# The levels of the gated linear attention over 53 slots instead of 36, in a two-layer encoder kernel

## The reference

```
bcum  = cumsum(log_a)                       # per key channel, log_a = log_sigmoid(...) / 16
a[t,s] = sum_d q[t,d] * k[s,d] * exp(bcum[t,d] - bcum[s,d])     for s <= t
o[t]   = a @ v   (and the part of earlier chunks, by a state)
y      = head_rms(o) * silu(r);  h = h + y @ w_out
```

## Time and profile before

| what | value |
| --- | --- |
| time, median of 3 runs | 2431.05 us (2427.83 to 2432.1) |
| profiled execution: time, span | 2430.49 us, 2428.8 us |
| mean granted TensorE clock | 0.992 |
| PE, DVE, ACT, POOL busy | 98%, 69%, 49%, 6% of the span |
| mean of `w_hi` (L542), `w_lo` (L922) | 1036 ns, 1204 ns |
| mean of the GLA's Exp (L868), of its 36 instructions | 1044 ns |
| GpSimd's subtractions (L490), multiplies (L499) | 72 in 61.7 us, 36 in 57.0 us |
| squares on ScalarE for a head (L853, two), Sqrt (L859) | 626 ns each, 478 ns |
| VectorE's evacuation in v_in (L943), r_in (L947) | 718 ns, 693 ns |

### The profile page before, as it was taken

One profiled execution on the slowest core, in us unless ns is written; L12 is line 12 of the kernel. 1 busy time (PEld: TensorE's weight loads), 2 busy tenths in 40 slices (PEclk: granted clock), 3 DMA queues, 4 the chain that ended last, 5 costly groups with the idle time before them and its releaser, 6 DMA issues.

```text
span 2428.8 us, 50438 instructions
## 1 busy us (share of the span) xinstructions
PE 2373.0 (98%) x19301; PEld 2286.6 (94%) x19301; DVE 1666.8 (69%) x2301; ACT 1198.6 (49%) x1540; POOL 152.7 (6%) x186
## 2 busy tenths in 40 slices
PE   8999989999999999999999899999999999999999
PEld 6998888999999999999999788999999999999998
DVE  5547796677755776577566788586777667766774
ACT  4344645555443444445458445554555445444543
POOL 0000001300000000000000556100000000000000
PEclk9999999999999999999999999999999999999999
DMA  6654455555565556665655333466556656666665
GB/s 180 189 149 124 129 144 124 169 171 190 176 205 183 187 184 194 188 198 180 190 170 165 105 96 97 123 196 205 178 187 199 206 182 206 201 196 193 207 192 164
DMA packets 430509, 420.25 MB, mean 173 GB/s; under 512 B 26067, under 2 KB 428285, under 8 KB 430365
## 3 DMA queue, kind: packets, MB, share of 16 engines
q1 hardware_dynamic: 416448, 415.29, 55.2%
q10 hardware_dynamic: 13932, 3.17, 1.2%
HBM read 416.31 MB, written 2.10 MB: 172 GB/s over the span
## 4 chain that ended last, share of the span: by engine, by line
PE 85%; DVE 7%; ACT 3%; issue 2%; POOL 1%; ACTq 1%; DMA 0%; DVEq 0%
PE ps L1419 26%; PE ps L1417 23%; PE ps L1418 23%; PE ps L1415 6%; DVE w_lo L922 2%; PE ps L1640 1%; ACT w_hi L542 1%; PE ps L1485 1%; PE ps L1484 1%; DVE gl_e L1256 1%; PE ps L1465 1%; POOL gl_e L490 1%; DVE rt L1120 1%; PE ps L1486 1%; DVE rt L1128 1%
## 5 line engine op out<-in xcount | busy, mean ns | idle before, releaser
L1417 PE MATMUL ps<-act_hi,w_hi 128*128 128x272 f32 (+1 forms) x4864 | 1371.1, 282 | 10.6 <-DVE w_lo L922 10.5
L1418 PE MATMUL ps<-act_lo,w_hi 128*128 128x272 f32 (+1 forms) x4864 | 1355.0, 279 | 0.0
L1419 PE MATMUL ps<-act_hi,w_lo 128*128 128x272 f32 (+1 forms) x4864 | 1354.7, 279 | 0.0
L922 DVE TENSOR_TENSOR w_lo<-raw,w_hi 128x1024 fp32r<-128x1024 f32 (+1 forms) x800 | 947.3, 1204 | 487.2 <-ACT w_hi L542 463.0
L542 ACT ACTIVATE w_hi<-raw 128x1024 fp32r<-128x1024 f32 (+1 forms) x797 | 816.4, 1036 | 673.3 <-PE ps L1419 641.2
L1417 PEld LDWEIGHTS ps<-act_hi,w_hi 128*128 128x128 f32 x4864 | 929.7, 191 | 18.8 <-issue 11.2
L1418 PEld LDWEIGHTS ps<-act_lo,w_hi 128*128 128x128 f32 x4864 | 929.7, 191 | 1.5
L1419 PEld LDWEIGHTS ps<-act_hi,w_lo 128*128 128x128 f32 x4864 | 929.2, 191 | 0.0
L1419 PE MATMUL ps<-g_both,w_lo 128*128 128x272 f32 (+1 forms) x1408 | 388.3, 276 | 0.0
L1419 PEld LDWEIGHTS ps<-g_both,w_lo 128*128 128x128 f32 x1408 | 268.2, 190 | 0.0
L1415 PE MATMUL ps<-g_both,w_hi 128*128 128x512 f32 x704 | 231.5, 383 | 0.0
(11 more groups left out here) (241 smaller groups left out, 1330.3 us busy)
## 6 DMA issues: line engine op xcount, KB each, us to landing
raw<-in_ffn_w_up SPq DMA_DIRECT2D x352, 512.0 KB, 4.6
raw<-in_ffn_w_down SPq DMA_DIRECT2D x128, 512.0 KB, 4.3
raw<-in_ab_w_in SPq DMA_DIRECT2D x96, 512.0 KB, 3.8
raw<-in_c_w_in SPq DMA_DIRECT2D x96, 512.0 KB, 3.8
raw<-in_ffn_w_down SPq DMA_DIRECT2D x64, 384.0 KB, 3.9
raw<-in_ab_w_out SPq DMA_DIRECT2D x32, 512.0 KB, 3.5
raw<-in_c_w_out SPq DMA_DIRECT2D x32, 512.0 KB, 4.4
tok<-in_x SPq DMA_DIRECT2D x4, 512.0 KB, 7.8
```

The costliest lines, as they stand in the source:

```text
L922: V.tensor_tensor(w_lo[:, s % 4, 0:kc * 256], raw[:, s % 4, 0:kc * 256], w_hi[:, s % 4, 0:kc * 256].bitcast(F32), ALU.subtract).then_inc(S ...
L1417: mm(o, wh, moving(xh, kk), start=(c == 0 and k == 0), stop=False)
L1418: mm(o, wh, moving(xl, kk), start=False, stop=False)
L1419: ins = mm(o, wl, moving(xh, kk), start=False, stop=end)
```

## The change

The levels get slots of their own in a pattern of three: two with a level, one without. Level v runs in slot 1 + v + v // 2, that is in slots 1, 2, 4, 5, 7, 8, ..., 52, 53. The slots of weighings and of squares are moved to come after their head's levels. The slots of Silu, of the normalisation and of the transposes stay as they are, and so do GpSimd's instructions. The engines' code reads the slot of a level from a table instead of using the slot as the level's number.

```diff
         GL_TICKS = 80
-        UNITS_AT = [([u - 1] if units[u - 1][1] is None else []) + [u] for u in level_units]
+        LEVEL_AT = {1 + v + v // 2: v for v in range(len(level_units))}
+        UNITS_AT = {t: ([level_units[v] - 1] if units[level_units[v] - 1][1] is None else []) + [level_units[v]]
+                    for t, v in LEVEL_AT.items()}
         GL_VT = {4 * (k + 1): (2 * k, 2 * k + 1) for k in range(8)}
-        WEIGH = {9: 0, 10: 1, 11: 2, 13: 3, 18: 4, 19: 5, 21: 6, 22: 7, 27: 8, 29: 9, 30: 10, 31: 11,
-                 36: 12, 37: 13, 38: 14, 39: 15}
-        SQUARE = {14: 0, 23: 1, 34: 2, 41: 3}
+        WEIGH = {15: 0, 17: 1, 18: 2, 19: 3, 29: 4, 30: 5, 31: 6, 33: 7, 42: 8, 43: 9, 44: 10, 45: 11,
+                 55: 12, 56: 13, 57: 14, 58: 15}
+        SQUARE = {21: 0, 35: 1, 47: 2, 60: 3}
 
 # ScalarE
-                    for v in ((0, 1) if t == 0 else (t + 1,)):
-                        if v < len(level_units):
-                            t0, t1 = level_span(units[level_units[v]][1])
-                            act.wait_ge(S("gl_dsub"), v + 1)
-                            act.wait_ge(S("gl_psub"), v + 1)
-                            e = gl_e[:, v % 2, :, :, t0:t1]
-                            A(e, e, ACT.Exp, scale=1.0 / GLA_TAU).then_inc(S("gl_exp"), 1)
+                    if t + 1 in LEVEL_AT:
+                        v = LEVEL_AT[t + 1]
+                        t0, t1 = level_span(units[level_units[v]][1])
+                        act.wait_ge(S("gl_dsub"), v + 1)
+                        act.wait_ge(S("gl_psub"), v + 1)
+                        e = gl_e[:, v % 2, :, :, t0:t1]
+                        A(e, e, ACT.Exp, scale=1.0 / GLA_TAU).then_inc(S("gl_exp"), 1)
 
 # VectorE
-                    for v in ((0, 1) if t == 0 else (t + 1,)):
-                        if v < len(level_units):
-                            sub(v)
-                    if t < len(level_units):
-                        mul(t)
-                    if t >= 1 and t - 1 < len(UNITS_AT):
-                        for u in UNITS_AT[t - 1]:
-                            take(u)
+                    if t + 1 in LEVEL_AT:
+                        sub(LEVEL_AT[t + 1])
+                    if t in LEVEL_AT:
+                        mul(LEVEL_AT[t])
+                    for u in UNITS_AT.get(t - 1, ()):
+                        take(u)
 
 # TensorE
-                    for u in (UNITS_AT[t] if t < len(UNITS_AT) else ()):
+                    for u in UNITS_AT.get(t, ()):
                         unit(u)
```

## The result

The changed kernel takes 2440.45 us (median of 7, 2436.41 to 2443.86) against 2431.16 us (7 runs). The ratio is 1.0039, with a 95% interval of 1.003 to 1.0048. The forecast was 2426.6 us with a range up to 2434.0: wrong in sign and outside the range.

What follows compares the result with a forecast made beforehand. TensorE, busy 98% of the span, was taken as the bound, so only its idle or lower-clock time could be won. Leaving 17.4 us, coming 13.5, net 3.9 off 2430.5: 2426.6 us, range 2421.0 to 2434.0.

Steps and rivals of the forecast that it cites:

- the pair: GpSimd's subtraction for the next level, then its multiply for this one; at odd levels both still fall within one step.
- the size of that pair: At odd levels, 1.34 + 1.34 to 2.15 + 1.82 us against 2.85 on offer; waits sum to 3.95 us.
- The covers: Work before odd levels hides GpSimd's lateness: no wait at 9, 27, 13, 21, 29; 0.3, 0.1, 0.3 at 3, 11, 19.
- The start: At the first levels: level 0 waits 2.6 us in place of 3.63, level 1 waits 1.0 for GpSimd; 3.6 together.
- the 2.03 that stay: Before step 1: TensorE's wait of 2.03 us for k_in's evacuation was to remain unchanged.
- Sqrt and Silu: ScalarE, slots 22, 36, 48: table loads ahead of an Exp soon needed; waits 0.6 (slot 36) and 1.2 (slot 48), sum 1.8.
- Level 34: VectorE, slots 50 to 53: normalisation work and slot 48's delay make multiply 34 late; wait 2.0 us, bounds 0 and 5.
- The clock: TensorE at its lower clock after waits at the start and level 34: 1.2 us, bounds 0 and 2 x 2.3.
- Turns: TensorE turning between kinds of matmul: 9 more turns, each 0 to 0.25 us; 0.7 us together.
- Even levels: GpSimd's 1.7 + 1.8 us fit into 5.8; levels 2, 8, 18, 26 meet an evacuation, 0.3 us together.
- Rival (b): Odd levels all pay today's 0.93 us wait, also behind transposes: 4 us more, 2430; chance 0.18.
- Rival (d): Table loads on ScalarE, slots 22, 36, 48: each of 7 holds it 1.3 us more, 9.1 us, 2435.7; chance 0.02.

Runs made afterwards that it cites:

- experiment 1: Changed kernel with GpSimd multiplying for an odd level before subtracting for the next one, instead of after: 2428.58 us, ratio 0.9989 to the kernel before.
- Experiment 4: Changed kernel with weighings and squares moved so that eleven stand in the slot right before an odd level: 2440.58 us, 1.0042 to the kernel before.
- experiment 7: The changed kernel itself, run and profiled again beside the kernel before: 2442.88 us, ratio 1.0044.
- experiment 5: Changed kernel, GpSimd multiplying first before odd levels, head 1's Silu and normalisation later (head 2's normalisation too): 2422.35 us; squares moved as well: 2416.88 us.
- experiment 2: Changed kernel with VectorE's weight-block split in v_in and r_in replaced by a one-input reciprocal of 176 elements: 2422.28 us, 0.9963 to the kernel before.

## Why the prediction was wrong

- **Where the pair stays** ("GpSimd is not touched, and that is the core"): right, and confirmed by experiment 1. All waits for GpSimd are at odd levels.
- **The step that failed** is the size of that pair: "its upper 2.15 + 1.82, against 2.85 on offer: a wait of 0 to 1.1. ... I take the middle", 3.95 us, with 1.0 for level 1. Measured at the same levels: 13.8. Single waits were 0.4 to 1.8. I had seen that the split now falls beside the subtraction, and took the longest row of before for its price. Two things were wrong with that. The middle was too low: at levels 5, 7 and 23 the pair took 3.8 to 3.9 us, close to my upper 3.97, and they waited 1.37, 1.36 and 1.37. And the bound was no bound: at levels 1, 3, 9, 17, 25 and 27 the pair took 4.0 to 5.1 us. The row of before has one split beside it, and in the changed kernel a second one can fall beside the multiply (2.31 us in place of 1.34 at level 3) or more than one VectorE instruction beside the subtraction. No row of before has such overlaps. From before alone, 2.6 us and one w_lo for each of the two splits that can fall beside the pair would have given 5.0 as the bound, an estimate that levels 3 and 27 reach (5.0 and 5.1).
- **The covers did not cover.** Level 3 behind transposes waited 1.77 (I gave 0.3), levels 9 and 27 behind the extra product 0.73 and 1.33 (I gave nothing). Against a pair of 4.6 to 5.1 us the 0.65 and 1.1 us are too little. Levels 11 and 19 stand behind the same transposes and did not wait: their pairs took 2.6 and 3.1. Levels 13, 21 and 29, behind weighings of 1.4 us, did not wait either, but their pairs took only 3.0, so the weighings were hardly put to the test there. Experiment 4 shows that they cover: its levels 23 and 29, with pairs of 3.9 and 4.0 us and a weighing in front, did not wait.
- **The start**: 0.78 + 1.53, or 2.45 and no wait at level 1 when the clock held (experiment 7). I gave 2.6 + 1.0; the 2.03 that stay were right.
- **Sqrt and Silu**: 0.6 and 1.2 forecast, 1.11 and 2.38 measured; level 15, which I had left to GpSimd, waited 0.97 for VectorE. Slot 22's Sqrt stands ahead of it, but it also went when GpSimd's order alone was turned (experiment 1) and VectorE's multiply there took 1.76 us beside GpSimd's, so both had a part. The places were right, and the sizes less than half: 1.8 against 4.5.
- **Level 34**: 2.0 forecast, 2.37 measured. With the normalisation moved away 0.98 of 1.97 stayed (experiment 5), so it is about half of the cause.
- **The clock**: 1.2 forecast, 4.9 measured. After 1.77 and 1.60 us it fell, where I had concluded from the earlier trace rows that 1.9 leaves it at 1.00.
- **Turns**: 0.7 forecast, 0.5 left over in the sum; not measured by itself.
- **Even levels** have two steps and wait little, as said: 0.47 at level 2, the rest only where other work stands in between.
- **Rival (b)**, the wait only moves, had the mechanism, but at 0.93 a level it was priced from the pair without splits beside it. **Rival (d)**, a drain behind each table load, is not there: slot 48's loads end at 1572.13 and 1573.92, and the next ACTIVATE starts 0.01 us later.

## What to carry to other kernels

Giving a pipeline more slots helps only as far as each queue's order lets an engine use them: look in every queue for an instruction that is ready but stands behind one that waits, and ask what hangs on the one that would move back. When a change shifts work of two engines against each other, price a shared resource by the overlap it will create, one length for each instruction that can fall beside it, and not by the longest row seen. And an engine's busy time says little about the time of the kernel: VectorE's 108 instructions for the levels took 28 us less here (93.4 to 65.2), as fewer of them ran beside GpSimd's, while the kernel got slower.

## What the runs showed of the hardware

- When a two-input VectorE instruction and one of GpSimd overlap, the one that starts later is stretched. Splits of 1.22 us that started ahead of GpSimd's multiply, or as its subtraction began, made these 2.31 and 2.71 us long, in place of 1.34 and 1.18, and kept their own 1.22. A split that started 0.24 us after GpSimd's multiply took 2.18, and the multiply kept its 1.34. VectorE's subtraction, two instructions, took 1.88 us when it came behind the start of GpSimd's multiply, and 0.52 to 0.78 us without it.
- Beside a one-input reciprocal of 1.24 us GpSimd's multiply kept 1.35 us (experiment 2).
- TensorE's clock fell to its lower level after waits of 1.60 and 1.77 us, and stayed up after 1.88 in the kernel before and after 2.38 and 2.37 in the changed one; in its second profile it fell after the same 2.37. The same wait of 2.02 before step 1 was followed by a fall at once in one execution of the changed kernel and not in the other. The length of one wait alone does not tell it.
